# Layer 0's front in another order: all sixteen modulation blocks summed ahead of the output projection, which runs in four parts

## The chip, the core and the metric

The kernel runs on one core of a Trainium2 chip. The metric is the device time of one execution in microseconds (us). The reader meets TensorE (PE), VectorE (DVE), ScalarE (ACT), GpSimd (POOL) and SyncE (SP), which here only issues DMAs.

## What is computed

One step of a two-layer trunk over 128 context tokens ("prompt", st 0) and 128 latent tokens ("sample", st 1), model width 1024. Layer 0 mixes tokens by a bidirectional RG-LRU, layer 1 by differential attention; each is followed by a mixture of experts (MoE) with 64 experts, 8 chosen per token. Cut to what matters for layer 0:

```
m  = silu(cond) @ mod_w + mod_b            # six vectors: shift, scale, gate, shift, scale, gate
h  = rms_norm(x, g0) * (1 + m[1]) + m[0]
xb = h @ w_in                              # (1024, 2560): first half -> gelu, second half -> conv
xr = centred_conv(xb[1280:])
r, i = sigmoid(block_diag(xr, gate_w) + gate_b)      # forward and backward
a = exp(-8 r softplus(-lam)); u = sqrt(1 - a^2) * (i * xr); scan both ways: h_t = a_t h_(t-1) + u_t
y = ((y_f + y_b) * gelu(xb[:1280])) @ w_out
x = x + m[2] * rms_norm(y, g1)
h = rms_norm(x, g2) * (1 + m[4]) + m[3]    # the MoE's input; its router is h @ router
x = x + m[5] * rms_norm(moe(h), g3)
```

## The kernel before

Every engine has a hand-written program of its own, in code order; semaphores tie them. Numbers in the MoE are fp32, and one fp32 matmul shows as two records in the trace. Large weights are loaded by SP in one queue, in code order, into `ring`, four slots of 24 KB per partition, and two more expert places. `PROLOGUE` lists each load of layer 0's front with its slot; a load may start once the slot's last reader is done (`mod_summed`, `win_done`, `gate_summed`).

**The front of layer 0** on PE, in code order:

- `sum_mod(m)`: block m of 512 columns of `mod_w` times silu(cond), eight matmuls. The 24 blocks are summed in groups (`MOD_GROUPS`), one PSUM bank per group (`MOD_BANKS`). Group 2 is blocks 4 to 11 (the mixer's gate and the MoE's shift and scale), group 3 is blocks 12 to 15. ACT copies a finished group to SBUF (`copy_mods`), PE turns it to columns (`turn_mods`), DVE adds the bias (`adaln_vectors`).
- `win("A"/"B", c)`: the conv half of `w_in`, ten chunks of 128 columns. ACT copies two chunks at a time, DVE does the conv, chunk by chunk (`xc_ready`).
- `gate(i)`, i = 0 to 39: the block-diagonal gates, forward r, forward i, backward r, backward i, ten each. Gates below 10 wait for DVE's conv; from the fifth on a gate waits for ACT's sigmoid of the gate five places before, which frees its bank. ACT works in the order 20 sigmoids, 20 `decays(0)` (tanh and exp), 20 sigmoids, 20 `decays(1)`, 20 roots, 10 gelus. So gate 25 waits for the first sigmoid after `decays(0)`.
- `gelu_in(c)`: the gelu half of `w_in`, ten chunks.
- `wout(st, first, end)`: the output projection of token half st over chunks first to end. Chunk 9 raises `mixer_done`.
- `norm_turn(1, b)`: transposes of the normalised x, two for each token half. They wait for a chain over ACT and DVE that starts at `mixer_done` of that half: ACT `rms_of_y`, DVE `residual_of`, ACT `rms_of_x`, DVE `normed`. DVE's `residual_of` also waits for gate gains, which go out to DRAM and come back spread over the partitions (`gains_loaded`).
- `shared_gate`, the router, transposes of plain h (`turn_plain`), and the first pass of the experts.

Blocks 4 to 7 are summed among the gates, 8 to 11 among the gelu chunks, 12 ahead of `wout(0)`, 13 between `wout(0)` and `wout(1)`, 14 and 15 after `wout(1)`.

**The MoE** runs 26 passes over expert buffers, six for gate and up weights, five for down weights. The first buffers are filled in the front; every later load waits for a pass to free its place (`refill`). The first of them are a down load that waits for `sh_summed` 1 and the loads behind pass 0.

Of the kernel before, what the change touches and what calls it, by code (L numbers as in the profile page):

```python
# [68 lines left out]
def column_ranks():  # L69
# [6 lines left out]
    for _ in range(ROUNDS):  # L76
        for kind in BODY:
# [137 lines left out]
def trunk(nc, a, outs, gains):  # L215
    y_prompt, y_sample, new_state, new_k, new_v = outs
    ctx = ExitStack()
    with ctx:
# [70 lines left out]
        mrow_late, mrow_last = (ring[:, q, 4096:6144].rearrange("p (b n) -> p b n", b=4) for q in (0, 3))  # L289
# [77 lines left out]
        GAIN_BANKS = (4, 6, 1)  # L367
# [55 lines left out]
        MOD_ROWS = [mrow_early[:, 0], mrow_early[:, 1], mrow_late[:, 0], mrow_last[:, 0], place4[:, 0:MB],  # L423
# [125 lines left out]
        def _(eng):  # L549
# [78 lines left out]
            def moe_loads(L, first):  # L628

                for e, free in first:  # L630
# [8 lines left out]
                    elif e in (14, 15):  # L639
                        load_mod(e)  # L640
# [123 lines left out]
            load_gates(1)  # L764
# [20 lines left out]
            for m in (11, 12):
                eng.wait_ge(s.mod_summed, m - 1)
                load_mod(m)
            eng.wait_ge(s.win_done, 1 + KR // 2 + KR)
            load_wout(1)
            eng.wait_ge(s.mod_summed, 12)  # L790
            load_mod(13)
            moe_loads(0, [(4, (s.state_ready, 1)), ("router", (s.q_ready, 2 * KR)), ("gains", (s.gains_stored, 16)),
                          (15, (s.mod_summed, 14)), (14, (s.wout_half, 1)), ("sh_gate", (s.wout_half, 1)),
                          (0, (s.mod_summed, 13)), (1, (s.mixer_done, 2)), ("in2", (s.mod_summed, 15)),
# [90 lines left out]
        def _(eng):  # L885
# [181 lines left out]
            for c in range(KR):  # L1067
                win("B", c)
# [17 lines left out]
            for c in range(5):  # L1086
                gelu_in(c)
# [1728 lines left out]
```

## Time and profile before

| | before |
|---|---|
| median of 3 runs | 1367.94 us (1367.43 to 1369.23) |
| the profiled execution, its own time | 1367.31 us |
| its span, first to last instruction | 1365.4 us |
| PE busy | 1294.4 us (95% of the span) |
| DVE, ACT, POOL busy | 463.0, 345.8, 18.1 us |
| DMA | 507.96 MB, mean 372 GB/s |
| mean granted TensorE clock | 0.987 of full speed |

Times in the rows are microseconds from the span's start. Busy shares are means over stages with different limits, so what a change in the front is worth is read from the front's own rows: which wait ends last there. Layer 0's front is the first 222 us or so.

### The profile page before, as it was taken

To read this page: it belongs to the slowest core of one execution; us is meant where nothing else is said; L and a number is where in the kernel's file an instruction comes from. 1 tells how busy PE (TensorE), PEld (TensorE's weight loads), DVE (VectorE), ACT (ScalarE), POOL (GpSimd) and SP (SyncE) were. 2 spreads that over 40 slices of the span, in tenths; PEclk is the share of its full clock that TensorE was granted. 3 is DMA by queue.
4 is the path that set the end of the run, shared out by engine and by line. 5 is a ranking of instruction groups with operands and counts; after the bars stand their busy time and mean duration, and the time that the engine had idled before them with its cause. 6 is when DMAs were issued, how large, how long until landed. Compare 5 with 4: busy or idle time off the path is not lost.

```text
span 1365.4 us, 25013 instructions
## 1 busy us (share of the span) xinstructions
PE 1294.4 (95%) x10086; PEld 681.9 (50%) x10086; DVE 463.0 (34%) x1185; ACT 345.8 (25%) x709; POOL 18.1 (1%) x23
## 2 busy tenths in 40 slices
PE   7989999999999999999989999999999999899896
PEld 5757646555544434443434554665544444344352
DVE  2556625333223222212231363432322322222223
ACT  2167033222122111211231254422121212111122
POOL 2100000000000000000000000000000000000000
PEclk9999999999999999999999999999999999999999
DMA  9796898999999999999999466889999999999993
GB/s 349 219 360 244 328 368 338 421 420 420 421 419 420 421 421 420 420 421 421 416 380 336 154 251 237 327 359 405 419 420 419 421 420 420 421 420 420 421 420 144
DMA packets 114513, 507.96 MB, mean 372 GB/s; under 512 B 19036, under 2 KB 27424, under 8 KB 64352
## 3 DMA queue, kind: packets, MB, share of 16 engines
q1 hardware_dynamic: 113136, 503.42, 92.0%
q0 software_dynamic: 1008, 2.45, 0.6%
q8 instruction: 83, 1.36, 0.4%
q10 hardware_dynamic: 256, 0.49, 0.1%
q14 instruction: 30, 0.25, 0.0%
HBM read 504.18 MB, written 2.14 MB: 371 GB/s over the span
## 4 chain that ended last, share of the span: by engine, by line
PE 67%; DMA 24%; DVE 4%; SPq 2%; ACT 2%; issue 1%; ACTq 0%; DVEq 0%
PE PS L887 65%; DMA ring<-in_moe_w_up 14%; DMA W<-in_moe_w_up 6%; DMA W<-in_mod_w 2%; DMA ring<-in_moe_w_down 2%; SPq L569 1%; DVE W L2257 1%; PE PS L1187 0%; DMA rows<-in_norm_g 0%; DVE hT L2092 0%; PE PS L1518 0%; ACT W L1826 0%; ACT W L1825 0%; PE PS L895 0%; DVE W L2254 0%
## 5 line engine op out<-in xcount | busy, mean ns | idle before, releaser
L887 PE MATMUL PS<-ring,W 128*32 128x512 f32 (+5 forms) x3400 | 583.9, 542 | 14.4 <-DMA W<-in_moe_w_up 9.2
L887 PE MATMUL PS<-W 128*128 128x128 bf16 (+7 forms) x3274 | 483.7, 358 | 17.4 <-DMA ring<-in_moe_w_up 13.4
L887 PEld LDWEIGHTS PS<-ring,W 128*32 128x32 f32 (+2 forms) x3400 | 196.0, 120 | 222.7 <-issue 195.0
L887 PEld LDWEIGHTS PS<-W 128*128 128x128 bf16 (+4 forms) x3274 | 236.7, 112 | 135.6 <-issue 115.9
L887 PE MATMUL PS<-W,junk 128*128 128x128 bf16 x848 | 116.5, 219 | 0.0
L2388 DVE TENSOR_TENSOR diag<-PS,diag 128x512 f32<-128x512 f32 x100 | 69.2, 692 | 139.0 <-ACT diag L1880 139.0
L887 PE MATMUL PS<-ring,hT 128*128 128x512 f32 x256 | 114.4, 596 | 1.1 <-DVE hT L2092 0.8
L887 PE MATMUL PS<-diag,W 128*128 128x512 bf16 (+2 forms) x424 | 112.6, 393 | 1.0 <-DVE diag L2632 1.0
L2382 DVE COPY W<-PS 128x512 f32<-128x512 f32 x53 | 36.7, 692 | 222.0 <-PE PS L887 222.0
L2365 DVE SCALAR_TENSOR_TENSOR W<-W,PS 128x256 f32<-128x256 f32 x52 | 25.0, 481 | 250.6 <-ACT W L1867 250.6
L1880 ACT CAST diag<-PS 128x512 bf16<-128x512 f32 x100 | 58.5, 585 | 190.5 <-PE PS L887 190.5
L1867 ACT ACTIVATE W<-PS 128x256 f32<-128x256 f32 x52 | 19.9, 383 | 316.3 <-PE PS L887 316.3
L887 PE MATMUL PS<-hT,ring 128*128 128x256 f32 (+1 forms) x384 | 81.6, 371 | 2.2 <-DVE hT L2092 2.2
L887 PEld LDWEIGHTS PS<-hT,ring 128*128 128x128 f32 x384 | 68.4, 193 | 18.0 <-issue 7.1
L887 PEld LDWEIGHTS PS<-ring,hT 128*128 128x128 f32 x256 | 46.9, 190 | 55.5 <-issue 53.5
L887 PEld LDWEIGHTS PS<-W,junk 128*128 128x128 bf16 x848 | 67.1, 98 | 11.4 <-issue 0.6
L887 PEld LDWEIGHTS PS<-diag,W 128*128 128x128 bf16 (+2 forms) x424 | 38.7, 103 | 67.3 <-issue 43.1
L1875 ACT COPY W<-PS 128x512 f32<-128x512 f32 x53 | 31.0, 585 | 137.1 <-PE PS L887 137.1
L2393 DVE TENSOR_TENSOR rows<-diag 128x1024 bf16<-128x1024 f32 x50 | 61.3, 1226 | 7.8 <-ACT diag L1882 7.8
L1882 ACT CAST diag<-diag 128x1024 bf16<-128x1024 f32 x50 | 52.3, 1045 | 37.9 <-DVE diag L2388 37.9
L887 PE MATMUL PS<-rows,W 128*128 128x512 bf16 x200 | 59.5, 379 | 0.0
L887 PE MATMUL PS<-ring,condT 128*32 128x512 f32 (+1 forms) x400 | 44.1, 565 | 0.0
(283 smaller groups left out, 825.2 us busy)
## 6 DMA issues: line engine op xcount, KB each, us to landing
ring<-in_moe_w_down SPq DMA_DIRECT2D x104, 1024.0 KB, 22.1
ring<-in_moe_w_gate SPq DMA_DIRECT2D x88, 1024.0 KB, 20.1
ring<-in_moe_w_up SPq DMA_DIRECT2D x88, 1024.0 KB, 23.9
W<-in_moe_w_gate SPq DMA_DIRECT2D x41, 1024.0 KB, 19.0
W<-in_moe_w_up SPq DMA_DIRECT2D x41, 1024.0 KB, 22.8
W<-in_moe_w_down SPq DMA_DIRECT2D x25, 1024.0 KB, 19.9
ring<-in_mod_w SPq DMA_DIRECT2D x28, 768.0 KB, 9.1
ring<-in_mod_w SPq DMA_DIRECT2D x16, 1024.0 KB, 12.1
```

The lines of the kernel that those rows point to most:

```text
L569: eng.dma_start(v[:, i, :], w.rearrange("(p k) f -> p (k f)", p=P)).then_inc(done, 16)
L887: return eng.matmul(out, lhsT, rhs, start=first, stop=last, skip_group_check=True)
L1867: eng.activation(sg, PS[:, 6, 0:F], ACT.Silu).then_inc(sg_.silu_ready, 1)
L1875: eng.copy(xg[:, 0:4, :].rearrange("p k n -> p (k n)"), PS[:, 6, :]).then_inc(sg_.xg_act, 1)
L1880: eng.copy(oparts[0][:, half * 512:(half + 1) * 512], PS[:, 4 + half, :]).then_inc(sg_.o_act, 1)
L1882: eng.copy(oparts[1], orest).then_inc(sg_.o_act, 1)
L2257: ins = eng.scalar_tensor_tensor(out=y, in0=xpad[:, c, :, t:t + P], scalar=conv_w(t, c), in1=y, op0=ALU.mult, op1=ALU.add)
L2365: eng.scalar_tensor_tensor(out=hE.rearrange("p (c q) -> p c q", c=2), in0=sg.rearrange("p (q c) -> p c q", c=2), scalar=wslot[:, 0:1], in1 ...
L2382: eng.tensor_copy(xg[:, 4:8, :].rearrange("p k n -> p (k n)"), PS[:, 7, :]).then_inc(sg_.xg_dve, 1)
L2388: eng.tensor_tensor(orest[:, cols], PS[:, 4 + half, :], oparts[0][:, cols], ALU.subtract)\
L2393: eng.tensor_tensor(oparts[2], orest, oparts[1], ALU.subtract).then_inc(sg_.o_dve, 1)
```

## The change

The order of the front changes on PE, and the order of SP's loads with it. ACT copies group 3 earlier, DVE takes the vectors of group 3 ahead of the residual, groups 2 and 3 swap their banks, and the router of either layer runs in two halves, st 0 ahead of st 1's last inputs. All blocks, matmuls and loads remain.

```diff
-MOD_BANKS = (0, 7, 4, 5, 6, 7, 6, 7)
+MOD_BANKS = (0, 7, 5, 4, 6, 7, 6, 7)
-            ("mod6", 1), ("mod7", 0), ("gel0", 2), ("gel1", 1), ("mod8", 0), ("mod9", 3), ("mod10", 0), ("wout0", 2),
-            ("mod11", 3), ("mod12", 0), ("wout1", 1), ("mod13", 3), ("mod14", 2), ("mod15", 3)]
+            ("mod6", 1), ("mod7", 0), ("mod8", 2), ("mod9", 1), ("mod10", 0), ("gel0", 2), ("gel1", 1), ("mod11", 0),
+            ("mod12", 3), ("mod13", 0), ("mod14", 3), ("mod15", 0), ("wout1", 3), ("wout0", 2)]
...
             load_gates(0)
-            load_gates(1)
             eng.wait_ge(s.mod_summed, 4)
             load_mod(4)
             eng.wait_ge(s.win_done, 1)
             load_mod(5)
+            load_gates(1)
+            load_gate_up(gate_place(5), a["moe_w_gate"][0, 5], a["moe_w_up"][0, 5], s.slot5_loaded)
             eng.wait_ge(s.win_done, 1 + KR // 2)
             load_mod(6)
...
+            for m in range(7, 11):
+                eng.wait_ge(s.mod_summed, m - 2)
+                load_mod(m)
             for j in range(2):
-                eng.wait_ge(s.mod_summed, 6 + j)
+                eng.wait_ge(s.mod_summed, 9 + j)
                 load_gel(j)
-            eng.wait_ge(s.mod_summed, 8)
-            load_mod(8)
+            eng.wait_ge(s.mod_summed, 11)
+            load_mod(11)
             eng.wait_ge(s.gate_summed, 4 * KR)
-            load_mod(9)
...
+            load_mod(12)
+            for m in (13, 14, 15):
+                eng.wait_ge(s.mod_summed, m - 1)
+                load_mod(m)
+            eng.wait_ge(s.mod_summed, 15)
+            load_wout(1)
             eng.wait_ge(s.win_done, 1 + KR // 2 + 5)
             load_wout(0)
...
+            moe_loads(0, [("in0", (s.mod_summed, FRONT)), ("down0", (s.mod_summed, FRONT)), ("in1", (s.win_done, gelus_in)),
+                          ("down1", (s.win_done, gelus_in)), (4, (s.state_ready, 1)), ("router", (s.q_ready, 2 * KR)),
+                          ("gains", (s.gains_stored, 16)), ("sh_gate", (s.wout_half, 1)), ("in2", (s.wout_half, 1)),
+                          (3, (s.mixer_done, 2)), ("sh_up", (s.x_new, 2))])
...
             for c in range(KR):
                 win("B", c)
+            sum_mod(4)
             eng.wait_ge(s.gate0_loaded, 16 * GATE_DMAS)
             for i in range(KR):
                 gate(i)
-            sum_mod(4)
+            sum_mod(5)
+            sum_mod(6)
             for i in range(KR, 2 * KR):
                 gate(i)
-            sum_mod(5)
+            sum_mod(7)
             eng.wait_ge(s.gate1_loaded, 16 * GATE_DMAS)
             for i in range(2 * KR, 2 * KR + 5):
                 gate(i)
-            sum_mod(6)
-            sum_mod(7)
-            for i in range(2 * KR + 5, 3 * KR):
+            sum_mod(8)
+            sum_mod(9)
+            for i in range(2 * KR + 5, 4 * KR - 5):
                 gate(i)
-            for i in range(3 * KR, 4 * KR):
+            sum_mod(10)
+            for i in range(4 * KR - 5, 4 * KR):
                 gate(i)
-            sum_mod(8)
...
+            for c in range(KR):
                 gelu_in(c)
-                if c < 9:
-                    gelu_in(c + 1)
-                    sum_mod(c // 2 + 8)
+                if c < 5:
+                    sum_mod(11 + c)
             turn_mods(2)
             eng.wait_ge(s.gelu_ready, KR)
-            sum_mod(12)
+            turn_mods(3)
...
             turn_gains(0)
+            wout(1, 0, 5)
             wout(0, 5, KR)
-            sum_mod(13)
-            wout(1, 0, 8)
+            wout(1, 5, 9)
             norm_turn(1, 0)
             norm_turn(1, 1)
-            wout(1, 8, KR)
+            wout(1, 9, KR)
             eng.wait_ge(s.rows_copied, 2)
-            sum_mod(14)
-            sum_mod(15)
...
             shared_gate(0, 0, 1)
+            router(0, 0)
+            eng.wait_ge(s.early_ready, 5)
+            turn_plain(0)
+            turn_plain(1)
             norm_turn(1, 2)
             norm_turn(1, 3)
-            turn_mods(3)
             norm_done(1)
```

What the program holds at three places of PE, before and after. Line 887 before is line 882 after (the matmul helper), 895 is 890 (`norm_turn`), 1281 is 1132 (`turn_plain`).

**After win B.** Before: the last forty matmuls of win B, then the first gates:

```order
L887 MATMUL PS<-hT,ring 128x256 x40
L887 MATMUL PS<-W 128x256 x3
L887 MATMUL PS<-ring,W 128x256
L887 MATMUL PS<-W 128x256
L887 MATMUL PS<-ring,W 128x256
L887 MATMUL PS<-W 128x256
```

After:

```order
L882 MATMUL PS<-hT,ring 128x256 x40
L882 MATMUL PS<-ring,condT 32x512 x8
L882 MATMUL PS<-W 128x256 x3
L882 MATMUL PS<-ring,W 128x256
L882 MATMUL PS<-W 128x256
L882 MATMUL PS<-ring,W 128x256
```

Eight matmuls on 32 rows, `sum_mod(4)`, now stand between win B and the first gate.

**Around the output projection.** Before, from the last gelu chunk (`hT,ring` x8) and `turn_mods(2)` (`con,ring`) to blocks 14 and 15:

```order
L887 MATMUL PS<-hT,ring 128x256 x8
L887 MATMUL PS<-con,ring 128x8x2 x4
L887 MATMUL PS<-ring,condT 32x512 x8
L887 MATMUL PS<-ring,W 128x512 x10
L1114 MATMUL PS<-con,hl 20x128
L907 MATMUL PS<-con,gg 32x128
L887 MATMUL PS<-ring,W 128x512 x10
L887 MATMUL PS<-ring,condT 32x512 x8
L887 MATMUL PS<-ring,W 128x512 x16
L895 MATMUL PS<-con,diag 128x128 x8
L887 MATMUL PS<-ring,W 128x512 x4
L887 MATMUL PS<-ring,condT 32x512 x16
```

After, from the last five gelu chunks:

```order
L882 MATMUL PS<-hT,ring 128x256 x40
L882 MATMUL PS<-con,diag 128x8x2 x4
L882 MATMUL PS<-con,diag 128x4x2 x4
L882 MATMUL PS<-ring,W 128x512 x10
L1107 MATMUL PS<-con,hl 20x128
L902 MATMUL PS<-con,gg 32x128
L882 MATMUL PS<-ring,W 128x512 x28
L890 MATMUL PS<-con,diag 128x128 x8
L882 MATMUL PS<-ring,W 128x512 x2
```

No block is left inside or behind the projection; both turns stand ahead of it, and one chunk of `wout(1)` instead of two follows the transposes of `norm_turn`.

**Up to the router.** Before, from `shared_gate` on (`hT,sq` is the router, `con,W 128x64` the logits):

```order
L887 MATMUL PS<-hT,ring 128x128 x16
L895 MATMUL PS<-con,diag 128x128 x8
L887 MATMUL PS<-con,ring 128x4x2 x4
L887 MATMUL PS<-hT,sq 64x256 x8
L887 MATMUL PS<-con,W 128x64 x2
L1281 MATMUL PS<-con,hT 128x128 x16
```

After:

```order
L882 MATMUL PS<-hT,ring 128x128 x16
L882 MATMUL PS<-hT,sq 64x128 x8
L1132 MATMUL PS<-con,hT 128x128 x8
L890 MATMUL PS<-con,diag 128x128 x8
L882 MATMUL PS<-hT,sq 64x128 x8
L882 MATMUL PS<-con,W 128x64 x2
L1132 MATMUL PS<-con,hT 128x128 x8
```

Half of the router and half of the plain transposes moved ahead of `norm_turn(1, 2)` and `(1, 3)`; `turn_mods(3)` left this place.

## Rows read from the trace of the kernel before

**Rows 1.** Windows of the span: length, busy time of each engine, PEclk, DMA share, GB/s

```profile
120.00:124.00 4.00, 4.00 (x20) 3.51 (x20) 3.83 (x11) 3.98 (x10) 0.00 (x0) 1.00 1.05 390
228.00:232.00 4.00, 4.00 (x38) 3.18 (x35) 0.48 (x1) 0.58 (x2) 0.00 (x0) 1.00 0.06 20
240.00:660.00 420.00, 406.78 (x3590) 197.18 (x3592) 120.23 (x269) 83.41 (x140) 0.00 (x0) 0.98 1.01 420
940.00:1340.00 400.00, 385.61 (x3393) 181.25 (x3391) 112.78 (x252) 79.72 (x134) 0.00 (x0) 0.99 1.01 419
```

**Rows 2.** Timeline of PE, first half of the front

```profile
46.28 19.19 PE L887 MATMUL PS<-hT,ring 128*128 128x256 f32 x80 [1.94 <-DVE hT L2092]
...
66.19 1.53 PE L887 MATMUL PS<-W 128*128 128x256 f32 x6 [0.72 <-issue]
...
73.80 0.67 PE L887 MATMUL PS<-W 128*128 128x256 f32 x2 [1.23 <-DVE ring L2265]
...
76.00 0.67 PE L887 MATMUL PS<-W 128*128 128x256 f32 x2 [1.10 <-DVE ring L2265]
...
77.89 1.92 PE L887 MATMUL PS<-ring,condT 128*32 128x512 f32 x16
...
100.41 1.56 PE L887 MATMUL PS<-W,ring 128*128 128x256 f32 x6 [1.82 <-ACT W L1815]
...
113.56 1.92 PE L887 MATMUL PS<-ring,condT 128*32 128x512 f32 x16
115.42 17.53 PE L887 MATMUL PS<-hT,ring 128*128 128x256 f32 x80
```

**Rows 3.** Timeline of PE, from the end of the gelu blocks to the router

```profile
156.21 0.96 PE L887 MATMUL PS<-con,ring 128*128 128x16 f32 x8
157.10 1.93 PE L887 MATMUL PS<-ring,condT 128*32 128x512 f32 x16
...
178.39 14.00 PE L887 MATMUL PS<-ring,W 128*128 128x512 f32 x32
192.23 1.04 PE L895 MATMUL PS<-con,diag 128*128 128x128 f32 x8
...
196.63 3.64 PE L887 MATMUL PS<-ring,condT 128*32 128x512 f32 x32
200.21 3.84 PE L887 MATMUL PS<-hT,ring 128*128 128x128 f32 x32
203.88 1.04 PE L895 MATMUL PS<-con,diag 128*128 128x128 f32 x8
...
206.56 1.95 PE L887 MATMUL PS<-hT,sq 128*64 128x256 f32 x16 [0.85 <-DVE hT L2092]
```

**Rows 4.** Timeline of ACT around the two layer 0 normalisations

```profile
177.83 1.28 ACT L1755 ACT_TABLE_LOAD   x1
...
196.74 1.02 ACT L1753 ACTIVATE junk<-PS 128x1024 f32<-128x1024 f32 x1 [1.93 <-PE PS L887]
...
208.54 0.37 ACT L1897 COPY W<-PS 128x256 f32<-128x256 f32 x1 [2.08 <-PE PS L887]
```

**Rows 5.** Timeline of DVE at the same place

```profile
182.71 0.16 DVE L2112 RECIPROCAL stat<-stat 128x1 f32<-128x1 f32 x1 [14.21 <-DMA ggb<-gains]
...
202.76 0.75 DVE L2083 TENSOR_SCALAR diag<-x,stat 128x1024 f32<-128x1024 f32 x1
```

**Rows 6.** SP's timeline, 112 to 115 us: one modulation block's load

```profile
113.66 1.43 SPq L563 DMA_DIRECT2D ring<-in_mod_w  x3
```

**Rows 7.** DMA issues of that window: KB each, median us to landing

```profile
ring<-in_mod_w SPq DMA_DIRECT2D x1, 512.0 KB, 7.0
```

**Rows 8.** One microsecond of the windows view, after PE's wait at 46 us

```profile
47.00:48.00 1.00, 1.00 (x4) 0.82 (x3) 0.00 (x0) 0.00 (x0) 0.00 (x0) 0.50 0.81 145
```

**Rows 9.** Timelines of PE and ACT at layer 1's router

```profile
853.81 2.90 ACT L1716 ACTIVATE hT<-PS,modT,amod 128x128 f32<-128x128 f32 x8 [0.77 <-PE PS L895]
...
856.96 1.95 PE L887 MATMUL PS<-hT,sq 128*64 128x256 f32 x16 [2.37 <-ACT hT L1716]
```

More of the change, by code:

```diff
@@ L783, in _ @@
+            eng.wait_ge(s.mod_summed, 15)
+            load_wout(1)
             eng.wait_ge(s.win_done, 1 + KR // 2 + 5)
             load_wout(0)
[L785 to L794, printed above, removed]
-                          (3, (s.mod_done, 5)), ("sh_up", (s.x_new, 2))])
+            gelus_in = 1 + KR // 2 + KR
@@ L1116, in _, with router, turn_plain @@
             turn_gains(0)
+            wout(1, 0, 5)
             wout(0, 5, KR)
-            sum_mod(13)
-            wout(1, 0, 8)
+            wout(1, 5, 9)
             norm_turn(1, 0)
             norm_turn(1, 1)
-            wout(1, 8, KR)
+            wout(1, 9, KR)
             eng.wait_ge(s.rows_copied, 2)
-            sum_mod(14)
-            sum_mod(15)
+            def router(L, st):
+                eng.wait_ge(s.router_loaded, 16 * (L + 2))
+                for k in range(KD):
+                    g = k % 2 * E
+                    ins = mm(PS[g:g + E, 4, st * P:(st + 1) * P], router_w[:, k, :], hT[:, k, st * P:(st + 1) * P],
+                             k < 2, k >= KD - 2)
+                return ins
+            def turn_plain(b):
+                st, half = divmod(b, 2)
+                for i in range(4):
+                    k = half * 4 + i
+                    ins = eng.matmul(PS[:, XM_BANKS[b], i * P:(i + 1) * P], hT[:, k, st * P:(st + 1) * P], ident,
+                                     start=i == 0, stop=i == 3, is_transpose=True, skip_group_check=True)
+                ins.then_inc(s.xm_turned, 1)
             def shared_gate(L, st, fc):
@@ L1268, in moe @@
                     eng.wait_ge(s.shared_gate_loaded, 32)
+                    router(1, 0)
                     norm_done(n)
-                eng.wait_ge(s.router_loaded, 16 * (L + 2))
-                w = router_w
-                for k in range(KD):
-                    g = k % 2 * E
-                    ins = mm(PS[g:g + E, 4, 0:T], w[:, k, :], hT[:, k, :], k < 2, k >= KD - 2)
-                ins.then_inc(s.router_summed, 1)
-                def turn_plain(b):
-                    st, half = divmod(b, 2)
-                    for i in range(4):
-                        k = half * 4 + i
-                        ins = eng.matmul(PS[:, XM_BANKS[b], i * P:(i + 1) * P], hT[:, k, st * P:(st + 1) * P], ident,
-                                         start=i == 0, stop=i == 3, is_transpose=True, skip_group_check=True)
-                    ins.then_inc(s.xm_turned, 1)
+                router(L, 1).then_inc(s.router_summed, 1)
                 def shared_in(w, bank, fc, first=0, end=KD):
@@ L1303, in moe @@
                 ins.then_inc(s.logits_done, 1)
-                if not L:
-                    eng.wait_ge(s.early_ready, 5)
-                for b in range(L, 4):
+                for b in range(1 if L else 2, 4):
                     turn_plain(b)
@@ L1850, in _ @@
             gelus(0, 5)
-            gelus(5, 9)
             copy_mods(2)
-            gelus(9, KR)
+            gelus(5, 7)
+            copy_mods(3)
+            gelus(7, KR)
             eng.wait_ge(s.u_ready, 2 * KR)
@@ L2344, in _ @@
                .then_inc(s.early_ready, 1)
+            eng.wait_ge(s.gains_loaded, 16)
+            residual_of(0, 0)
+            normed(1, 0)
+            input_of(1, 0)
+            residual_of(0, 1)
+            normed(1, 1)
+            input_of(1, 2)
             def one_hots(sg_, item, j, buf):
```

24 lines of the change are left out of this document (2 added, 22 removed).

## The prediction, made before the changed kernel ran

> **What bounds the kernel now.** I read the windows first. From 240 to 660 us and from 940 to 1340 us the DMA share is 1.01 at 419 to 420 GB/s [rows 1]: the expert weights stream without a gap, so either MoE ends a fixed time after its stream restarts. What restarts it? Between 228 and 232 us the share is 0.06 [rows 1]. All first buffers are full, and nothing more can be loaded until PE's first pass frees a place. So layer 0's front counts by one thing: when PE reaches pass 0. A microsecond there is a microsecond of the whole. Faster loads in the front buy nothing, unless PE waits for one.
>
> The timeline of PE then shows the front as a chain of work with few waits. Win B starts at 46.28 and ends at 65.5. The gates wait 0.72 us for ACT's copy of win B, then 1.23 and 1.10 us for DVE's conv; gate 25 waits 1.82 us for ACT, which has `decays(0)` to do first [rows 2]. From 100.41 to `norm_turn(1, 2)` at 203.88 there is no wait at all [rows 2, 3]. Behind it the router waits for the last inputs, and from there routing sets the pace [rows 3].
>
> **The change, part by part.** Unit prices: a block is 113.56 to 115.42 us, 1.86; a gate (100.41 to 113.56, fifteen of them) 0.88; a gelu chunk 17.53 for five, 3.5 [rows 2]; a turn of modulations 156.21 to 157.10, 0.89; a chunk of `wout` 178.39 to 192.23 for eight, 1.73 [rows 3].
>
> *Block 4 ahead of the gates.* PE is free at 65.5. The block fills the 0.72 us wait and puts gates 0 to 6 later by 1.1 us, ending at 73.4. Gate 7 still starts at 73.80 and gate 8 at 76.00, when DVE is ready, and gate 9 ends at 77.89 as before [rows 2]. Block 4 is free: 1.86 us won. The cover is the conv wait; without it the block would cost its 1.86.
>
> *Blocks 5 and 6 behind gate 9*, where one block stood: +1.86. Gates 10 to 19 end that much later, so ACT's sigmoids, its `decays(0)` and its next sigmoid are as late, and gate 25 starts at 102.3 instead of 100.41. Between gates 19 and 25 stand three blocks as before, so the wait of 1.8 us stays. **+1.86.**
>
> *Gate 25 to the end of `wout(1)`.* Before, blocks 8 to 13 lie here, after, blocks 10 to 15: six each. `turn_mods(3)` is added: **+0.89.** Blocks 14 and 15 used to stand behind `wout(1)`, under the normalisation of st 1, where they cost little; that cover is given up.
>
> *A new wait at `norm_turn(1, 0)`.* Before, DVE starts the st 0 residual at 182.71, held up 14.21 us by the gains [rows 5], while PE still has chunks to do. In the new order `wout(1, 0, 5)` goes first, and `mixer_done` of st 0 comes at about 190 instead of 176.5 (178.39 less block 13): 1.86 from above, 0.89, one block more ahead of it, and five chunks, 13.3 in all; then PE has only four chunks, 6.9 us. The chain from `mixer_done` to the normalised x takes, on st 1, 196.74 (ACT) to 203.5 (DVE's last step, 202.76 and 0.75) [rows 4, 5], 6.8 us; on st 0 add the table load of 1.28 us [rows 4] and 0.15 us to start: 8.2. PE waits **+1.3.** Behind it are `norm_turn(1, 1)` and the last chunk, on which `mixer_done` of st 1 hangs. The gains leave PE 4.6 us later (1.86, 0.89 and a block), so they land near 187; DVE wants them at 192.7, when ACT's first step of the chain is done. Hidden.
>
> For that table load the Trainium skill (ScalarE: Activation LUTs, "What ACT_TABLE_LOAD costs") gives about 2.66 us for each switch, as a drain of about 1.38 us comes with it. By the page the new wait would be 2.7 us and the total 1.4 us more. The row has 1.28 us, so I take the row.
>
> *Behind `mixer_done` of st 1.* Before, two blocks and `shared_gate` take 196.63 to 203.88, 7.25 us, a little longer than the 6.8 of the chain [rows 3]. After, `shared_gate` (3.67), half a router (1.0) and two plain transposes (0.95) make 5.6, less than the chain, which then decides: 6.9. **-0.35.** `turn_mods(3)` leaves the place behind `norm_turn`; PE waited 0.85 us there anyway, for ACT.
>
> *The router.* Its 256 columns take 206.56 to ACT's copy at 208.54 [rows 3, 4]. Only half is left after the last inputs. **-0.97** (the bounds are 0, if the small matmuls don't scale, and 1.0). In layer 1 the same: PE waits 2.37 us there for ACT's two input halves (853.81, 2.90 us) and the router starts at 856.96 [rows 9]; the first half is ready at 855.3, so its matmuls fit in the wait. **-0.97.** ACT's copies, DVE's vectors and the swapped banks lie in the idle time of engines that nobody waits for: 0.
>
> *Loads.* A block's load into a quiet queue takes 7.9 us from its first issue to its last landing: three issues in 1.43 us [rows 6], the last piece 7.0 us [rows 7]. At 390 GB/s [rows 1] 2.1 MB take 5.4 us, so loads in a row come every 5.4. Blocks 11 to 15 come on PE every 3.5 + 1.86, also 5.4 us, from only two slots. Block 11's load is freed by block 10; then PE has five gates and one gelu chunk, 4.4 + 3.5 = 7.9 us. Margin: none, but no loss either. I take 0; the bounds are 0 and 3 us. Block 6 must land by 79.7: from about 52 us on, three blocks and an expert's 2.1 MB are 21.5 us, and the twenty small gate DMAs have 4 us. The expert weights are in by about 213 us, before pass 0 at 225.
>
> Sum at pass 0: 1.86 + 0.89 + 1.3 - 0.35 - 0.97 = +2.7 us. Layer 1: -0.97. Together **+1.8 us**. The profiled execution took 1367.31 us (span 1365.4), so one like it takes 1369.1; the median lies 0.6 above it, so for the median I say **1369.7 us**, 0.13% more. What this kernel's measurement tells from no change is about 0.2%, 2.7 us.
>
> **The rivals.**
>
> *Forecast*, +1.0 to +2.7: chance 0.50.
>
> *The clock falls at the router* (slower). After the wait of 1.94 us that ends at 46.28 the granted clock went from 1.00 to 0.50, 2.4 to 1.2 GHz, within a microsecond of work [rows 2, 8]. The new order makes PE wait 1.3 us ahead of `norm_turn(1, 2)` and 1.7 us behind it, with 1 us of work between, and router, logits and ranks follow. Against it: gaps of 1.82 us at 100 and 1.23 and 1.10 us at 74 to 76 left it at full [rows 2]. Three microseconds at half clock cost up to 1.6: +3.4, 1371.3. It decides from 0.9 us on. Chance 0.12. The Trainium skill (TensorE: Matmul & The Clock Gate, "What's actually happening") also knows only full and half rate, and has activity release the throttle; the row agrees.
>
> *PE waits for a block*: block 6, or 11 to 15 with their margin of nothing. One to three microseconds: +2.8 to +4.8, 1371.6. Chance 0.17.
>
> *The page's table load*: +3.2, 1371.1. Chance 0.02, as the row speaks against it.
>
> *Nothing is lost in the front*: the two new waits are hidden by something I misplace, or the first buffers decide and not PE. The quiet 228 to 232 us speak against it. -1 to +0.9, 1367.9. Chance 0.12.
>
> *All waits close.* The four waits of [rows 2] make 4.87 us. Filled wholly, with 0.89 and 1.95 us of work now ahead of `norm_turn(1, 2)`: -2.0, and twice -0.97: -4.0, 1364.0. But gate 25 must wait for ACT. Chance 0.07.
>
> **How the numbers follow.** Faster by over 0.2%: 0.07. Slower: 0.12 + 0.17 + 0.02 and the upper edge of the forecast, 0.33. Same: 0.60. The range takes in the forecast, the case of no loss and most of the slower ones, up to +4.6: 1366.8 to 1372.5, with under 2 in 10 outside. The forecast alone spans 1368.9 to 1370.6.
>
> **What would show it.** In the changed profile: no wait at 66 us; gate 8 still at 76.0; gate 25 near 102.3 with a wait near 1.8 for ACT; PE unbroken from there to about 197; a wait of 1.3 us at `norm_turn(1, 0)` for DVE; `mixer_done` of st 1 near 200.8; the last half of the router ending near 211.3; pass 0 near 225, and a DMA gap before it of 10 us or more. Layer 1's router should end 1 us sooner after its inputs. A wait for `ring<-in_mod_w` in PE's list, or PEclk under 1.00 between 205 and 220 us, makes me wrong upward; gate 25 before 101.5 downward.

## The result, and the profile after

The changed kernel takes **1380.1 us** (median of 4 runs, 1377.58 to 1382.42) where the kernel before took 1367.85 in the same batch (4 runs, 1367.43 to 1369.23): ratio 1.0081, 95% interval 1.0065 to 1.0098. It is slower by 12 us; I had said 1369.7 and at most 1372.5. The profiled execution took 1382.42 us, span 1380.6, against 1367.31 and 1365.4; the mean granted clock was 0.98, before 0.987.

First the landmark on which I had put everything, pass 0, and the way to it. PE's timeline of the changed kernel (start, duration, instruction, and in brackets the idle time before it with its releaser), first half of the front:

```profile
46.92 19.19 PE L882 MATMUL PS<-hT,ring 128*128 128x256 f32 x80 [1.94 <-DVE hT L2091]
66.04 1.93 PE L882 MATMUL PS<-ring,condT 128*32 128x512 f32 x16
...
76.64 0.67 PE L882 MATMUL PS<-W 128*128 128x256 f32 x2 [1.10 <-DVE ring L2264]
...
82.61 1.93 PE L882 MATMUL PS<-ring,condT 128*32 128x512 f32 x16 [2.15 <-DMA ring<-in_mod_w]
...
105.12 1.56 PE L882 MATMUL PS<-W,ring 128*128 128x256 f32 x6 [1.81 <-ACT W L1814]
...
124.88 1.93 PE L882 MATMUL PS<-ring,condT 128*32 128x512 f32 x16 [1.04 <-DMA ring<-in_mod_w]
...
130.64 1.93 PE L882 MATMUL PS<-ring,condT 128*32 128x512 f32 x16 [0.18 <-DMA ring<-in_mod_w]
...
137.48 1.93 PE L882 MATMUL PS<-ring,condT 128*32 128x512 f32 x16 [1.27 <-DMA ring<-in_mod_w]
```

Set beside [rows 2]: block 4 stands at 66.04 with no wait, as forecast, and gate 8 starts 0.64 later than before, just as much as win B does. So block 4 was free. (That win B starts later is no part of the change: e6 and e11 below are one program, and start it at 46.20 and 47.03.) Then come four waits that the kernel before has not, all for a modulation block's weights: block 6 at 82.61, blocks 11, 12 and 13 behind the gelu chunks. They make 4.64 us. Gate 25 is at 105.12 instead of 100.41.

The second half, from the last part of the output projection to pass 0:

```profile
178.30 24.20 PE L882 MATMUL PS<-ring,W 128*128 128x512 f32 x56
203.90 1.09 PE L890 MATMUL PS<-con,diag 128*128 128x128 f32 x8 [1.40 <-DVE diag L2082]
204.83 1.88 PE L882 MATMUL PS<-ring,W 128*128 128x512 f32 x4
206.79 3.81 PE L882 MATMUL PS<-hT,ring 128*128 128x128 f32 x32
...
213.57 1.09 PE L890 MATMUL PS<-con,diag 128*128 128x128 f32 x8 [0.93 <-DVE diag L2082]
216.31 1.09 PE L882 MATMUL PS<-hT,sq 128*64 128x128 f32 x16 [1.64 <-DVE hT L2091]
...
231.23 1.08 PE L882 MATMUL PS<-ring,W 128*64 128x256 f32 x8
```

The wait of 1.40 us ahead of `norm_turn(1, 0)` is the new one that I had priced at 1.3. The router's last half takes 1.09 us where the whole took 1.95 [rows 3]. Pass 0 starts at 231.23. In the kernel before it starts at 222.24:

```profile
222.24 1.95 PE L887 MATMUL PS<-ring,W 128*64 128x256 f32 x16
```

So **+9.0 us** at pass 0, and not +2.7. And still the stream of weights has to wait for PE there; windows of the changed kernel (length, busy time of each engine, PEclk, DMA share, GB/s):

```profile
64.00:72.00 8.00, 8.00 (x45) 5.58 (x44) 7.41 (x19) 3.64 (x6) 0.00 (x0) 1.00 0.56 110
72.00:116.00 44.00, 38.71 (x220) 25.28 (x219) 18.33 (x45) 24.94 (x54) 0.00 (x0) 1.00 1.04 390
200.00:204.00 4.00, 2.60 (x7) 0.86 (x6) 2.17 (x4) 1.44 (x3) 0.00 (x0) 1.00 0.00 2
216.00:220.00 4.00, 3.23 (x29) 2.96 (x30) 1.02 (x12) 2.02 (x6) 0.00 (x0) 0.82 0.74 250
220.00:224.00 4.00, 4.00 (x9) 0.99 (x7) 3.62 (x28) 3.54 (x8) 0.00 (x0) 0.75 0.01 5
230.00:240.00 10.00, 9.38 (x86) 6.21 (x84) 4.21 (x17) 0.38 (x1) 0.00 (x0) 1.00 0.00 0
```

They show two more things. Between 64 and 72 us, just when block 6 was to be loaded, the DMA engines had work for only 0.56 of the time; from 72 us on they were full. And behind the router, from 216 us, the granted clock is below 1.00, at the place where I had put a rival.

Why was the DMA share low? SP's timeline of the changed kernel:

```profile
49.88 3.74 SPq L562 DMA_DIRECT2D ring<-in_mod_w  x6
53.67 14.40 SPq L725 DMA_DIRECT2D ring<-in_lru_gate_w  x20
68.11 1.67 SPq L568 DMA_DIRECT2D W<-in_moe_w_gate  x1
69.83 0.43 SPq L568 DMA_DIRECT2D W<-in_moe_w_up  x1
70.31 26.40 SPq L562 DMA_DIRECT2D ring<-in_mod_w  x15
```

SP had twenty small transfers of the backward gates to issue, of 4 to 100 KB each. They occupied it for 14.4 us, 0.72 each; meanwhile the engines worked off what was queued ahead of them, the loads of blocks 4 and 5 (share 1.03 and more from 52 to 64 us), and then ran short of work. In the kernel before the same twenty took

```profile
50.25 10.52 SPq L728 DMA_DIRECT2D ring<-in_lru_gate_w  x20
```

Behind them, in program order, came 2.1 MB of expert 5. So block 6's load, whose place was free when win B ended at 66.0, was issued at 70.31 and landed at 82.6. PE wanted it at 80.46.

The sum at pass 0, from these rows: win B started 0.64 later; one block more ahead of gate 25, 1.93; block 6, 2.15; blocks 11 to 13, 2.49; `turn_mods(3)`, 0.93; the wait at `norm_turn(1, 0)`, 1.40; then 0.46 in many steps of a tenth; the last normalisation -0.33; from there to pass 0, -0.7, the router's half. Together 9.0. The fall of the clock behind the router cost nothing at pass 0 in this execution: e2, below, needs the same 17.67 us from `norm_turn(1, 2)` to pass 0 with the clock at 1.00 throughout as the changed kernel with its fall (17.66); what PE loses, it would have waited for DVE (0.77 us in e2).

Layer 1's router did what was forecast. Its first half now lies in the wait:

```profile
868.69 1.09 PE L882 MATMUL PS<-hT,sq 128*64 128x128 f32 x16 [0.83 <-DVE hT L2091]
870.08 1.09 PE L882 MATMUL PS<-hT,sq 128*64 128x128 f32 x16 [0.30 <-issue]
```

The changed kernel starts blocks 21 and 22 13.3 us later than the kernel before and layer 1's pass 0 12.3 us later, so 1.0 is won between them. But then +9.0 and -1.0 make +8.0, and the span is 15.2 longer. The other 7 us lie where the program was not touched, and there the clock differs. The profiled execution is also the slowest of the four. At 816 us:

```profile
816.35 1.97 PE L1581 MATMUL PS<-con,W 128*128 128x128 f32 x8 [2.50 <-DVE W L2723]
```

The kernel before has the same wait of 2.50 us at 806.11, and the eight transposes behind it take 1.09 us.

### The profile page after: what moved, and what is told of

The parts are those of the page before. It is cut to its first block, busy times and chain, and to the rows that moved or that the text cites. A ratio compares the mean times of both kernels' runs of the same rounds, so it can differ in the third digit from the quotient of the medians.

```text
span 1380.6 us, 25077 instructions
## 1 busy us (share of the span) xinstructions
PE 1303.5 (94%) x10118; PEld 687.2 (50%) x10118; DVE 463.4 (34%) x1185; ACT 346.4 (25%) x709; POOL 18.2 (1%) x23
## 4 chain that ended last, share of the span: by engine, by line
PE 64%; DMA 24%; SPq 6%; DVE 2%; ACT 2%; issue 2%; ACTq 0%; DVEq 0%
PE PS L882 62%; DMA ring<-in_moe_w_up 16%; DMA W<-in_moe_w_up 4%; SPq L568 2%; SPq L725 2%; DMA ring<-in_mod_w 2%; DMA W<-in_mod_w 2%; SPq L562 1%; PE PS L1200 0%; DMA rows<-in_norm_g 0%; PE PS L890 0%; SPq L571 0%; PE PS L1517 0%; ACT W L1825 0%; ACT W L1824 0%
## 5 line engine op out<-in xcount | busy, mean ns | idle before, releaser
L882 PE MATMUL PS<-W 128*128 128x128 bf16 (+7 forms) x3274 | 485.4, 359 | 14.7 <-DMA ring<-in_moe_w_up 12.4
```

The lines of the kernel that those rows point to most:

```text
L882: return eng.matmul(out, lhsT, rhs, start=first, stop=last, skip_group_check=True)
```

## The experiments

**The theories.** A: the front is longer because PE waits for blocks that are issued late (block 6) or whose slots come round too late (11 to 13). B: the order itself is dearer than my sum. C: the clock falls in waits that the new order makes or moves, at the router and later. D, a rival to all: any shift of the stages behind pass 0 costs more than its size, whatever makes it.

Runs e1 to e4 shared a chip (before there: 1368.35 us median, 12 runs), e5 to e8 another batch (1369.41, 35 runs), e9 to e11 a third (1368.55, 23 runs).

**e1, expert 5's load behind block 7's.** The changed kernel with one load moved.

```
             load_gates(1)
-            load_gate_up(gate_place(5), ...)
             ...
                 load_mod(m)
+                if m == 7:
+                    load_gate_up(gate_place(5), ...)
```

> The changed kernel, with one load moved: expert 5's gate and up weights go out behind block 7's load instead of ahead of block 6's. Loads theory (PE waited 2.15 us for block 6 because SP issued its load 4.8 us later than its slot came free and 2.1 MB of expert weights stood ahead of it): the wait goes, gate 25 starts near 103.0 instead of 105.1, pass 0 comes about 2.1 us sooner, near 229.1, and the median falls by about 2 us, to 1378. Rival (the block's own size and the order on PE set the pace, the load is late only in name): pass 0 moves by under 0.5 us.

1375.97 us (6 runs, 1373.25 to 1376.65), ratio 1.0048 [1.0031, 1.0066]. Block 6's wait is gone. Block 6's load was issued at 68.33 instead of 70.31, still behind the gates. Waits for blocks 9, 11 and 15 (0.46, 2.29 and 0.38 us) are there. `norm_turn(1, 2)` starts at 210.57, 3.0 us earlier than in the changed kernel; 0.8 of them it had already at gate 8, ahead of block 6, so the load order is worth about 2.2. Then the clock fell: the router's last half takes 1.97 us instead of 1.09, and pass 0 is at 229.54, only 1.7 earlier.

**e2, blocks 11 to 15 spread over all ten gelu chunks.**

```
-                if c < 5:
-                    sum_mod(11 + c)
+                if c % 2:
+                    sum_mod(11 + c // 2)
```

with `copy_mods(3)` behind all gelus and `wout0` loaded ahead of `wout1`.

> The changed kernel, with blocks 11 to 15 each behind every second gelu chunk (1, 3, 5, 7, 9) instead of behind each of the first five; the same work on PE. Loads theory (two slots give a block every 5.4 us at best, and PE asks for one every 5.4): with 8.9 us between blocks the waits of 2.5 us for ring<-in_mod_w vanish, pass 0 near 228.7, median 2.5 us lower. Rival (the waits are an effect of bandwidth that the expert loads then take elsewhere): the waits turn up at wout or at the gelu chunks, and pass 0 moves by under 1 us.

1376.91 us (1374.05 to 1379.87), 1.0055 [1.0036, 1.0074]. No wait for blocks 11 to 15 is left. Pass 0 is at 230.46, only 0.8 earlier: in this execution block 6 waited 3.39 us, the clock fell behind that wait, and block 6 took 3.37 us for 1.92. At the router PE has the same waits as in the changed kernel, and here the clock does not fall:

```profile
212.79 1.09 PE L890 MATMUL PS<-con,diag 128*128 128x128 f32 x8 [0.92 <-DVE diag L2081]
215.53 1.09 PE L882 MATMUL PS<-hT,sq 128*64 128x128 f32 x16 [1.64 <-DVE hT L2090]
```

```profile
216.00:220.00 4.00, 3.54 (x27) 1.97 (x23) 1.74 (x19) 2.59 (x7) 0.00 (x0) 1.00 0.58 191
```

**e3, both.**

> Both edits of the two runs before. Loads theory: they add, pass 0 near 226.6, that is +4.3 us against the kernel before; what stays is the order's own price, forecast as +2.7 at pass 0 before the changed kernel ran. Median near 1375.5 if the later stages stay as in the changed kernel's runs, near 1371 if their extra comes and goes with the clock. Rival (the order costs the 9 us at pass 0 by itself): pass 0 stays above 229.

1375.93 us (1372.05 to 1378.89), 1.0047 [1.003, 1.0063]. The head of PE's list of waits up to 222 us:

```profile
PE PS L911 <- DMA rows<-in_norm_g: 8.3, 1, 8.3
PE PS L883 <- DVE hT L2091: 3.9, 3, 1.9
PE PS L891 <- DVE diag L2082: 2.3, 2, 1.4
PE PS L883 <- ACT W L1815: 1.8, 1, 1.8
PE PS L883 <- DVE ring L2264: 1.3, 2, 1.1
```

No block is waited for, and gate 25 is at 102.65. `norm_turn(1, 2)` starts at 208.40, 5.2 us earlier than in the changed kernel. At pass 0 (227.41, +5.2) only 3.8 of them are left, because the clock fell in between: the stretch takes 19.01 us, where e2 at full clock has 17.67. So A is worth about 5 us, and of the 5.2 that stay the clock took 1.3. The timeline of e3 at the router:

```profile
208.40 1.09 PE L891 MATMUL PS<-con,diag 128*128 128x128 f32 x8 [0.92 <-DVE diag L2082]
211.13 1.63 PE L883 MATMUL PS<-hT,sq 128*64 128x128 f32 x16 [1.64 <-DVE hT L2091]
213.23 1.12 PE L883 MATMUL PS<-con,W 128*128 128x64 f32 x4 [0.46 <-ACT W L1896]
214.14 1.91 PE L1133 MATMUL PS<-con,hT 128*128 128x128 f32 x8
215.84 3.14 PE L883 MATMUL PS<-junk,both 128*128 128x512 bf16 x4
```

Eight transposes of plain h take 1.91 us where in the kernel before sixteen take 1.92. Its windows have the clock at 0.50, the lower level of 1.2 GHz:

```profile
212.00:216.00 4.00, 3.54 (x21) 3.07 (x18) 1.21 (x15) 1.99 (x5) 0.00 (x0) 0.50 0.45 154
```

**e4, the kernel before and 80 transposes of the identity behind block 15.** A delay and nothing else, to test D: `keep_clock(4, 80)`.

> The kernel before, with 80 transposes of the identity on PE behind blocks 14 and 15, about 9 us of work that nobody reads; no load and no other instruction is moved. It tells what a bare delay of the front is worth at the end. Theory one to one: pass 0 about 9 us later and the median 9 us higher less at most 1 us, 1376 to 1377, with the runs as close together as those of the kernel before. Clock rival (a shifted front meets TensorE's clock falls elsewhere, and the changed kernel's 3 us beyond pass 0's come from that): the median is 11 to 13 us higher, the runs scatter by 4 us or more, and PEclk is low in one more place of layer 1.

1379.49 us (1377.13 to 1380.45), 1.0073 [1.0056, 1.009]. Pass 0 is at 230.57, +8.3 (8.7 from gate 25 on, as gate 25 was 0.4 early), and the median is +11.1. A pure delay of the size of the changed kernel's gives nearly the changed kernel's time, so that pass 0 sets the end is right. The 2.4 us on top of 8.7 are not clear of the noise: the interval of the ratio is 7.7 to 12.3 us.

**e5, the router's halves alone**, in the kernel before: `router(0, 0)` behind `turn_mods(3)`, `router(1, 0)` ahead of layer 1's `norm_done`, and `router(L, 1)` in the old place.

> The kernel before with one part of the change alone: the router's product in two halves, the first half (8 matmuls) ahead of the wait for the second half's transposes, in layer 0 behind turn_mods(3) and in layer 1 behind the shared gate's wait; order, banks, loads and blocks are those of before. The parts add up (my theory): the half is hidden in the wait of 0.85 us ahead of the router in layer 0, so pass 0 comes at about 221.4 (-0.8), layer 1's router is 1.0 us shorter as in the changed kernel, the end is -1.8, about 1366.5. Rival, the router's halves let the clock fall there (in the changed kernel and in the three kernels derived from it the granted clock is 0.75 to 0.82 just behind router(0,1)): then the logits and rest products behind it take 1.88 to 3.1 us a group instead of 1.88, pass 0 comes at 223 or later and the gain of layer 0 is gone. Rival, any shift of the later stages brings clock falls worth 2 to 3 us as in the kernel with a pure delay: about 1369.

1368.45 us (12 runs, 1366.74 to 1372.72), 0.9995 [0.9982, 1.0009]: 1 us less in the medians, which the interval doesn't separate from nothing. In the profile pass 0 is 0.3 earlier though this execution was 0.6 later at gate 25 (100.98), so -0.85; layer 1's part is again 1.0. No clock falls at the router here: PE has no wait ahead of it.

**e6, blocks where waits are**: the kernel before with block 4 ahead of the gates, 5 and 6 where 4 and 5 stood, 7 and 8 behind gate 24, and e5's router.

```
+            sum_mod(4)
             eng.wait_ge(s.gate0_loaded, 16 * GATE_DMAS)
             for i in range(KR): gate(i)
-            sum_mod(4)
+            sum_mod(5)
             ...
-            sum_mod(6)
             sum_mod(7)
+            sum_mod(8)
```

Block 8's old place ahead of the gelus is empty; it goes to slot 2 ahead of `gel0`, and expert 5's load behind block 9's. The two banks are swapped as in the changed kernel.

> The kernel before with what the change's parts seem to be worth having and nothing else: block 4 in the wait ahead of gate 0, blocks 5 and 6 where 4 and 5 stood, 7 and 8 behind gate 24, so that no block stands between the gates and the gelus; block 8 and its load in another place, expert 5's load behind block 9's, the two banks swapped, and the router in halves as in the run beside it. Blocks 9 to 15 and the output projection stay. The number of blocks ahead of gate 25 that wait there stays four, so gate 25 should come at 100.4 and the gelus at 113.6 instead of 115.4: pass 0 at about 219.6 (-2.7), the end at -3.6, about 1364.5. If the loads are late (the rival that decided the changed kernel): a wait at block 4, 6, 8 or gelu 0 that shows by name. If any shift costs clock: about 1367.

1367.61 us (12 runs; eleven from 1362.19 to 1371.48 and one of 1918.39 at a mean granted clock of 0.654, which hardly moves the median), 0.999 [0.9976, 1.0004]. Its PE timeline:

```profile
65.19 1.92 PE L887 MATMUL PS<-ring,condT 128*32 128x512 f32 x16
73.59 0.67 PE L887 MATMUL PS<-W 128*128 128x256 f32 x2 [0.23 <-DVE ring L2271]
75.79 0.67 PE L887 MATMUL PS<-W 128*128 128x256 f32 x2 [1.10 <-DVE ring L2271]
...
100.20 1.56 PE L887 MATMUL PS<-W,ring 128*128 128x256 f32 x6 [1.82 <-ACT W L1821]
```

No load is late, gate 25 is where it was, and a block has been won. Pass 0 is at 219.36, -2.9, against -2.7 expected; counted from gate 25 it is -2.67. The median doesn't show it: the interval holds 1.

**e7, the waits at the router covered.** e3 with work put into the idle time, none of the waits taken away:

```
             turn_plain(1)
+            keep_clock(5, 8)
             norm_turn(1, 2)
             norm_turn(1, 3)
+            keep_clock(5, 14)
             norm_done(1)
```

> The changed kernel with both load repairs (pass 0 at 227.41), and 8 transposes of the identity (0.83 us) in the wait of 0.92 us ahead of norm_turn(1,2) and 14 (1.46 us) in the wait of 1.64 us ahead of router(0,1), where TensorE stands idle. They add work and take no wait away. If the clock fell there because TensorE stood idle, it stays at full speed: the group of 16 matmuls of router(0,1) takes 1.09 instead of 1.63 us, the rest products 1.88 instead of 3.14, and pass 0 comes about 1.5 us earlier, at 225.9, near the 224.9 forecast plus the 0.5 of the fall at 46 us. If the fall has another cause, pass 0 stays at 227.4 or comes later by what the transposes cover badly.

1372.07 us (12 runs, 1369.02 to 1373.88), 1.0018 [1.0006, 1.0029], against 1.0047 [1.003, 1.0063] for e3: 22 useless transposes make the kernel 3 to 4 us faster. The timeline:

```profile
208.78 1.09 PE L891 MATMUL PS<-con,diag 128*128 128x128 f32 x8
209.71 1.69 PE L997 MATMUL PS<-con 128*128 128x128 f32 x14
211.52 1.09 PE L883 MATMUL PS<-hT,sq 128*64 128x128 f32 x16
213.07 0.66 PE L883 MATMUL PS<-con,W 128*128 128x64 f32 x4 [0.46 <-ACT W L1898]
213.57 1.04 PE L1133 MATMUL PS<-con,hT 128*128 128x128 f32 x8
214.58 2.07 PE L883 MATMUL PS<-junk,both 128*128 128x512 bf16 x4
```

and the window that had 0.50:

```profile
212.00:216.00 4.00, 3.54 (x27) 1.96 (x23) 1.75 (x19) 2.60 (x7) 0.00 (x0) 1.00 0.56 192
```

From `norm_turn(1, 2)` to pass 0 it takes 17.58 us (208.78 to 226.36), e3 19.01: 1.4 us at this place. Pass 0 is at 226.36; in this execution block 9 waited 2.5 us for its load, and win B ran at full clock (17.50 us instead of 19.19).

The profiles alone show that the fall needs the waits, not that the waits always bring it: of four with the waits open, three have it (the changed kernel, e1, e3) and one has not (e2); of two with the waits covered (e7, and e9 below) none has it. Firmer is the mean granted clock of every execution: 0.978 to 0.984 in the seven of e3, 0.986 to 0.990 in the twelve of e7, and 0.984 to 0.990 in the twelve of the kernel before beside e3. The two batches don't explain it, as the kernel before has the slightly lower clock in e7's. C is shown: with the waits covered the clock is higher in every execution.

**e8, a delay of 20 transposes** in the kernel before, where e4 had 80.

> The kernel before with 20 transposes of the identity behind sum_mod(15): 2.1 us more work, placed where the run with 80 of them had its 8.3. That run ended 2 to 3 us later than its delay at pass 0. If each us at pass 0 costs one at the end, 1370.0. If the end of the kernel before is a lucky phase of the clock, which any shift loses, 1372 to 1373.

1371.1 us (12 runs, 1368.55 to 1376.53), 1.0015 [1.0001, 1.0029]. Pass 0 +2.6, the median +1.7. D falls in its strong form: a small shift costs about its own size (the interval is 0.1 to 4.0 us). There is no lucky end in the kernel before that any shift would lose.

**e9, the changed kernel as it is with e7's 22 transposes.**

> The changed kernel as it is, loads and all, with the 22 transposes of the run e7 alone: 8 ahead of norm_turn(1,2), 14 ahead of router(0,1). If the idle waits ahead of the router make the clock fall there, the group router(0,1) is 1.09 us at full clock, the stretch from norm_turn(1,2) to pass 0 is 17.6 us as in e7 instead of 19.0 in the run with both repairs, and with the waits for loads as they are pass 0 is 0 to 1.5 us earlier than 231.23 (the router was at full clock in the changed kernel's profile and fell just behind it, so less than in e7 is to be won). The median would be 1 to 4 us below the changed kernel's 1380.1. If e7's gain over the run with both repairs (1372.07 against 1375.93) was not from the cover, the median stays at 1380.

1378.76 us (5 runs, 1376.97 to 1380.82), 1.0076 [1.0062, 1.009], 1.3 below the changed kernel's median from another batch, with overlapping intervals. In the profile pass 0 is at 230.47, 0.8 earlier, which is just what its three waits for blocks are shorter (3.9 us instead of 4.6). From `norm_turn(1, 2)` it takes 17.57 us, the changed kernel 17.66: where the fall had cost nothing, the cover wins nothing at pass 0. The times don't separate the two kernels.

**e10, e6 with a wait of layer 1 covered**: `keep_clock(6, 20)` ahead of `turn_o(0)`, in the wait of 2.50 us behind which the changed kernel's clock fell.

> The kernel of e6 (blocks in the waits, router in halves) with 20 transposes of the identity (2.1 us) in the wait of 2.50 us ahead of turn_o(0) in layer 1, the wait behind which the changed kernel's clock fell at 816 us (turn_o 1.97 instead of 1.09 us) and that of before and of e6 did not. If that wait brings the fall in a part of the executions, the median is up to 2 us below that of e6 run beside it, and the scatter smaller. If not, it is the same within 1 us.

1366.66 us (11 runs, 1362.44 to 1368.31), **0.9988 [0.9978, 0.9997]**, the only kernel here whose interval excludes that of no change on the faster side, though by less than the 0.2% that I had set as the bound. The cover works:

```profile
799.03 2.41 PE L1001 MATMUL PS<-con 128*128 128x128 f32 x20
801.60 1.09 PE L1588 MATMUL PS<-con,W 128*128 128x128 f32 x8 [0.17 <-DVE W L2731]
```

**e11, e6 again**, beside e10.

> The same kernel as e6, again: its interval against before held 1 (0.9976 to 1.0004) with a scatter of 8 us. The profile gave pass 0 2.9 us earlier and layer 1's router 1.0 us shorter, so 3.9 us at the same clock, a ratio of 0.9972; a ratio of 0.9985 to 0.999 as in the first run would mean that more than half of it is lost to clock falls.

1367.58 us (12 runs, 1363.09 to 1372.81), 0.9988 [0.9973, 1.0003], as the first time. This execution shows the fall that e10 covers:

```profile
805.82 1.94 PE L1588 MATMUL PS<-con,W 128*128 128x128 f32 x8 [2.50 <-DVE W L2730]
```

The medians of e10 and e11 differ by 0.9 us, and the slowest of e10 is 1368.31, of e11 1372.81. The two ratios are the same, 0.9988, and e10's interval is only narrower. That the fall goes with this wait is seen in the profiles; what the cover is worth in time is not shown.

**All profiles together.** "Beyond" is what the span grew beyond pass 0's shift (for kernels with the router in halves, 1.0 is added, as layer 1 is that much shorter). "Clock lost" is counted behind pass 0: over windows of 5 us, the sum of 5 times (1 - PEclk); placing the windows otherwise moves a row by some 2 us. The last column is the mean granted clock of all executions of the kernel, without e6's one of 1918 us.

| kernel | gate 25 to pass 0 | pass 0 | span | beyond | clock lost | clock, all executions |
|---|---|---|---|---|---|---|
| before | 121.83 | 222.24 | 1365.4 | | 14.3 | 0.9880, 0.9865, 0.9876 |
| changed | 126.11 | 231.23 | 1380.6 | +7.2 | 23.6 | 0.9825 |
| e1 | 127.54 | 229.54 | 1372.2 | +0.5 | 14.4 | 0.9852 |
| e2 | 123.42 | 230.46 | 1375.9 | +3.3 | 14.4 | 0.9852 |
| e3 | 124.76 | 227.41 | 1377.0 | +7.4 | 23.7 | 0.9813 |
| e4 | 130.52 | 230.57 | 1378.1 | +4.4 | 18.3 | 0.9860 |
| e5 | 120.98 | 221.96 | 1366.3 | +2.2 | 17.3 | 0.9863 |
| e6 | 119.16 | 219.36 | 1360.3 | -1.2 | 10.5 | 0.9846 |
| e7 | 123.91 | 226.36 | 1368.5 | 0.0 | 12.4 | 0.9877 |
| e8 | 123.98 | 224.86 | 1369.7 | +1.7 | 12.5 | 0.9866 |
| e9 | 125.34 | 230.47 | 1376.9 | +4.3 | 17.1 | 0.9854 |
| e10 | 119.18 | 217.79 | 1360.5 | +0.6 | 14.1 | 0.9865 |
| e11 | 119.15 | 220.32 | 1365.8 | +3.3 | 14.5 | 0.9848 |

The kernel before has three clocks, one for each batch: beside e1 to e4, e5 to e8, e9 to e11. The two kernels with the largest surplus have the largest clock loss, and e6 is least in both; it is not one to one (e2, e11). The profiled executions are not typical either: the changed kernel's and e3's are the slowest of their four and seven, e6's and e10's the fastest of their twelve and eleven.

The same program also moves. e6 and e11 are one kernel with spans of 1360.3 and 1365.8, and e10 is the same up to layer 1. Their pass 0 lies at 219.36, 220.32 and 217.79, but from gate 25 to pass 0 the three agree to 0.03 us. So the scatter of the front lies ahead of gate 25, and in the front it is the stretch behind it that one profile can compare.

Over all executions the clock is a better witness than in one. The changed kernel's four go from 1377.58 us at a mean clock of 0.985 to 1382.42 at 0.980. Carried on along that line to the 0.987 of the kernel before, that gives about 1375.6, which is an estimate: 7.8 us above 1367.85, where pass 0 and layer 1's router make 8.0. The rest of the 12.2 would then be clock.

## Why the prediction was wrong

**What bounds the kernel: right.** Pass 0 sets the end. The DMA share is 0.00 from 230 to 240 us, and the delays of 2.6 and 8.3 us cost 1.7 and 11.1. An earlier pass 0 went with medians 1.0 to 1.9 us lower in e6, e10 and e11, of which only e10's is clear of no change.

**The step that failed is the term *Loads*, taken as 0 with a bound of 3; it was 4.6 us of waits**. Without them (e3) the changed kernel's `norm_turn(1, 2)` comes 5.2 us earlier, and pass 0 3.8, as e3 lost 1.3 more to the clock. It has two halves.

*Block 6.* I had counted bytes and given "the twenty small gate DMAs" 4 us. I had left out that SP must issue them: it was busy with them for 14.4 us, and block 6's place came free at 66.0, in the middle of 53.67 to 68.07. From 64 to 72 us the engines were at 0.56, so 3.5 us of their time were lost; my budget ended at 77.5 (52 and 21.5 and 4), and with these 3.5 it ends at 81.0, past the 79.7 of my own deadline. I had the row for it: the kernel before has the same twenty issues in 10.52 us on SP's timeline. I read that timeline only around 112 us [rows 6]. Expert 5's two loads, ahead of block 6's in program order, did the rest: e1 moves only them, SP is as busy as before (14.50 us), and the wait is gone. So neither half alone is shown to make a wait: no run has the expert's load ahead and the small ones elsewhere.

*Blocks 11 to 13.* "Margin: none, but no loss either" took the price of a load into a quiet queue, and left no place for a late one. Here the queue was not quiet. Block 11's load, issued at 115.93, landed at 124.88: 8.95 us where I had 7.9 (the last piece took 8.0 us, 7.0 in [rows 7]). Block 13's took 10.6 us, from 126.87 to 137.48. The blocks waited 1.04, 0.18 and 1.27 us. Where two slots turn at just the pace of PE, each late landing is a wait that nothing gives back. e2, with a block every 8.9 us (two chunks and the block before it) instead of 5.4, has none. The rival *PE waits for a block* was this mechanism, at "one to three microseconds" and a chance of 0.17. A margin of nothing should have made this the likeliest case.

**The order's own price: near.** Without load waits (e3) gate 25 is at 102.65, against 102.3. `turn_mods(3)` cost 0.93 against 0.89. The wait at `norm_turn(1, 0)` was 1.40 against 1.3: it comes from `mixer_done` of st 0 moved behind five chunks of st 1, and the gains were hidden as said. By the Trainium skill (ScalarE: Activation LUTs, "What ACT_TABLE_LOAD costs"), with 2.66 us a switch, it would have been 2.7. The trace doesn't agree: in the changed kernel the load takes 1.28 us from 196.85, and ACT's next step starts right behind it, at 198.15. The end of st 1's chain was -0.33 against -0.35. At full clock e3 would reach pass 0 at 226.0 (227.41 less e7's 1.43), +3.7 where I had +2.7. Half of the missing 1.0 is no price of the order: win B starts at 46.81 in e3 and at 46.28 before, which is within the scatter of one program. The rest is small steps behind gate 25. That gate 25 came so near is partly luck, since gate 8 starts at 74.20 in e10 and 75.79 in e6, the same program up to there: in e10 the clock did not fall behind the wait at 46 us (win B takes 17.50 us), in e6 it did (19.06).

**The router's halves: right.** -0.85 in layer 0 (e5) and -1.0 in layer 1, against -0.97 for each. In the changed kernel's order it is -0.7 in layer 0, and in e2 too, where the clock is full: PE then waits 0.77 us for DVE further on, 0.45 in the kernel before.

**The rival *the clock falls at the router*: it happened, and with chance 0.12 I held it too small.** It came in three of the four profiles that have the waits open. In the changed kernel's it cost nothing at pass 0, in e1's and e3's 1.3 us, which is near the "up to 1.6" I gave it, and in e2's it did not come. (Where I wrote ahead of e5 that all three kernels derived from the changed one had the clock at 0.75 to 0.82 there, that is wrong for e2.) Against it I had put that waits of 1.1 to 1.8 us left the clock at full in [rows 2]. These stood alone; at the router two waits of 0.92 and 1.64 us lie 1 us of work apart, and a third of 0.46 behind. The Trainium skill (TensorE: Matmul & The Clock Gate, "What's actually happening") has TensorE's clock throttled by default and released by activity. e7 agrees: the same program with more to do in its waits stayed at 1.00, window 212 to 216, where e3 had 0.50.

**What I did not foresee at all**: clock falls far behind the change. By the estimate from the four executions they make up the difference between +8.0 (pass 0 and layer 1's router) and the median's +12.2. The falls at the router (e3, e7) and ahead of `turn_o(0)` (e10, e11, the changed kernel) follow waits of PE and were absent where the waits were covered; e7's gain of 3.9 us on e3, of which pass 0 explains 1.1, hints that more hangs on them than their own place.

**What stays open.** Why the changed kernel and e3 lose more clock behind pass 0 than e1 and e7 do is not settled. It is not the chance of one profile: all seven executions of e3 have a mean clock of 0.984 or less, all six of e1 0.984 or more. So e3 reaches pass 0 2.1 us before e1 and ends no earlier (1375.93 and 1375.97). e4's 2.4 us over its delay, where e8 has none, are within the noise. No run covers the wait at 46 us.

## What to carry to other kernels

Before moving a load, lay the issuing queue's own timeline beside the time when the load's place comes free: small transfers cost issue time (here 0.5 to 0.7 us each) beside their bytes, and whatever stands ahead in program order comes first. A schedule whose loads keep pace with "no margin" loses; give each at least the scatter of a landing, here one to two microseconds (block 6's wait was 1.98, 2.15 and 3.39 us in three profiles with the same loads). Piling independent work ahead of a chain of dependent steps takes away that chain's cover twice: the waits appear, and then the clock can fall in them. Useful work in such a wait pays, and in e7 even useless work did. And compare single profiles only over the stretch that repeats, here from gate 25 to pass 0; for the rest take the times and clocks of all executions.

## What the runs showed of the hardware

- Twenty small transfers took SP 10.5 us to issue in the four profiles with nothing large just ahead (before, e4, e5, e8), 0.53 us each, and 14.4 to 15.4 us in the nine where two modulation blocks of 2.1 MB were queued just ahead of them, 0.72 us each and more.
- The granted clock fell behind idle times of 1.64 to 3.39 us in some executions of a program and not in others. The same wait of 2.50 us: the transposes behind it take 1.09 us in the kernel before and in e6's first profile, 1.97 and 1.94 in the changed kernel's and e11's. The same wait of 1.94 us at 46 us: win B takes 19.19 us before and 17.50 in e10. In windows of 5 us a fall shows as 1.7 us of clock lost in e11 (0.66 from 805 to 810), and as 3.4 in the changed kernel (0.50 and 0.83 from 816 to 826).
- A fall of the clock right behind the router cost nothing at pass 0 in the changed kernel (17.66 us from `norm_turn(1, 2)`, 17.67 in e2 without a fall) and 1.3 us in e3.
- Twenty-two transposes with no use raised the mean granted clock of every execution (0.978 to 0.984 in e3, 0.986 to 0.990 in e7) and made a kernel 0.3% faster (1.0047 to 1.0018).
